# A hybrid HGRN2, convolution and MoE layer: first gather in four passes, x1 kept in DRAM by channels, squares summed on GpSimd, expert input turned by transposes, order of experts first

## Chip, cores and metric

The kernel runs on one core of a Trainium2 chip. The metric is the device time of one execution in microseconds (us), the median of several. In the text PE is TensorE, DVE is VectorE, ACT is ScalarE, POOL is GpSimd, and SP is SyncE, which issues nearly all DMAs. All times inside an execution are counted from the start of the profiled span.

## The reference, cut to what matters

One layer over 256 tokens (128 context tokens, s = 0, and 128 latent tokens, s = 1) of width 1024:

```
h   = rmsnorm(x) * (1 + scale1) + shift1
mix = (g_a * y_a + g_b * y_b) @ w_out                 # HGRN2 branch and convolution branch
x1  = x + gate1 * mix
h   = rmsnorm(x1) * (1 + scale2) + shift2
scores  = sigmoid(h @ w_router)                       # 64 experts, 8 groups
combine = top-8 of the 4 best groups, scores / sum * 2.5
act    = silu(h @ w_gate[e]) * (h @ w_up[e]) * combine[e]      # per expert e, width 256
routed = sum over e of act @ w_down[e]
shared = (silu(h @ ws_gate) * (h @ ws_up)) @ ws_down
out = rmsnorm(x1 + gate2 * (routed + shared)) * final_norm_g
```

Everything is fp32. Each expert has 3 MB of weights, so the 64 experts bring 192 loads of 1 MB.

## The kernel before

**Stages.** The text calls x after the first residual x1. Up to about 392 us the mixers run; their last products are the two halves of the output projection, `project_split("wo0")` and `("wo1")`. DVE adds them to `x_t` (x1 by channels: partition = channel, `[128, 8, 256]`) and writes `h_t` = x1 times the gain of the second norm. Then comes the routing stage, and from about 422 us to 890 us the expert stage, then a short tail (second residual, final norm, store).

**Routing stage on PE** (lines 1793 to 1920). In program order: `sum_squares(j)`, j = 0 to 3, adds the squares of x1 over the channels, four products with a single column each; ACT makes the squares in two buffers `tmp`, and the third and fourth square wait until PE has used the first ones. `sum_squares(0)` stands between the two output projections. Then `router(k)`, k = 0 to 7, the logits (64 columns each); `gained_to_tokens(j)`, 16 products with the identity that turn `h_t` to tokens; `add_shift(j)`, four 512-column products that add the shift row divided by the RMS, in the same PSUM banks; five kinds of small products that count the tokens of each expert (`cnt_ready`); `x1_to_tokens(j)`, 16 transposes of `x_t`, copied by ACT to `x1_out` and stored in DRAM by SP; `gather(part)`, part = 0 to 3, which selects the tokens of the first two steps from `h_hi` and `h_lo` (the expert input split in two fp32r parts) with the one-hot matrix `sel_p`; the product that puts the experts in order (`order_ready`); `turn(0)`.

**DVE there** runs the top-8 selection (up to `mask`), then `h_rest(j)`, which writes `h_lo`, for j = 0 and 1, the positions, `one_hots(0)` (`built`), `h_rest(2)` and `(3)`, the weights `comb`, the keys that rank the experts (`hot_done`), the table of extra slots (`nx_done`), the copy of the order to `e_row` (`order_done`), and two of the four copies of the gathered tokens to `xg`. ACT does the other two.

**Expert stage.** 26 steps; a step takes 1, 2 or 4 experts side by side (`STEPS`). The six experts of the first three steps are fixed, and their weights are loaded before routing is known. Chunk numbers count the loads of 1 MB; there are 18 places in SBUF, and load n goes into the place of load n - 18 once PE has used that (`freed`: `gu_done` for gate and up weights, `dn_done` for down weights). SP issues the loads in that order, so it waits for the release of one place before it issues the next. Chunks 18 and 19 need the order of experts and `gu_done` 1 (first half of `gate_up(0)`); 20 and 21 `gu_done` 2; 22 and 23 `dn_done` 2 (end of `down(0)`); 24 to 27 `gu_done` 3 and 4 (`gate_up(1)`); 28 and 29 `dn_done` 4 (end of `down(1)`).

A step n on PE is: `gate_up(n)` in two halves; `last_results` (scatter of the step before); `act_to_channels(n)`, which waits for ACT's silu and DVE's product `act_r`; `second_turn` or `gather_next`; `down(n)`. In step 0 the small products `before_tables` (which end with `spread2`, the RMS spread over partitions for the shared expert) come after the first half of `gate_up(0)` and `item_tables` after the second.

**Tail.** After the last step DVE signals `loop_done`, PE scatters the last results (8 products), and DVE multiplies by gate2 and adds x1, which SP has loaded back from DRAM behind the last weights.

Release of the places, of the kernel before (the waits that pace the loads):

```
                if part == 2:
                    sp.wait_ge(dn_done, 2 * step + 2)
                else:
                    sp.wait_ge(gu_done, 2 * step + 1 + part)
```

## Time and profile before

| what | us |
|---|---|
| median of 3 runs | 904.22 |
| lowest, highest | 902.78, 906.89 |
| the profiled execution | 905.2 |
| its span | 903.4 |
| PE busy | 831.0 (92%) |
| DVE, ACT, POOL busy | 387.5, 215.3, 91.6 |
| DMA over the span | 284.70 MB, mean 315 GB/s |
| main DMA queue, share of 16 engines' span | 80.5% |
| mean granted TensorE clock | 0.968 |

In a row of the timeline the first two numbers are the start and the time in us, `x16` is the number of instructions merged, and the bracket gives the idle time of the engine before them and who ended it. An fp32 product gives two MATMUL records, an fp32 transpose one. In a row of windows the stretch is followed by its length, the busy time of PE, PEld (weight loads), DVE, ACT and POOL with their instructions, the granted clock of TensorE (1.00 is 2.4 GHz, 0.50 is 1.2 GHz), the DMA share and GB/s.

### The profile page before, as it was taken

How to read it: one execution, taken by the hardware profiler on the slowest of the kernel's cores; microseconds unless marked ns; L12 is line 12 of the kernel's file. 1: busy time of each engine (PE TensorE's matmuls, PEld its weight loads, DVE VectorE, ACT ScalarE, POOL GpSimd, SP SyncE). 2: the span in 40 equal slices, each digit the busy share in tenths (PEclk: the TensorE clock that was granted, in tenths of full speed). 3: DMA queues.
4: the chain of work that ended last, by engine and by line, in shares of the span. 5: the costliest groups of instructions: out<-in, count | busy, mean ns of one | idle time of the engine just before them, and what ended most of it. 6: DMA issues, size and time to landing. Idle time of an engine off the chain costs nothing.

```text
span 903.4 us, 12822 instructions
## 1 busy us (share of the span) xinstructions
PE 831.0 (92%) x5242; PEld 561.4 (62%) x5242; DVE 387.5 (43%) x760; ACT 215.3 (24%) x335; POOL 91.6 (10%) x63
## 2 busy tenths in 40 slices
PE   4699999999899999998999999779999999899973
PEld 2388989569899988995535544435554755345221
DVE  1225898369799846736232322111212111112104
ACT  3124443133354334403111111101111101011001
POOL 1000536205243310000000000000000000000000
PEclk9899999999899999979999999979999999999987
DMA  8979878135234538973999999999999999999993
GB/s 316 386 253 338 309 268 317 39 103 174 67 123 135 193 110 268 410 301 119 377 378 418 418 416 415 418 416 417 416 417 410 418 414 417 417 417 417 418 400 142
DMA packets 81173, 284.70 MB, mean 315 GB/s; under 512 B 5208, under 2 KB 11736, under 8 KB 64728
## 3 DMA queue, kind: packets, MB, share of 16 engines
q1 hardware_dynamic: 80760, 283.11, 80.5%
q8 instruction: 43, 0.70, 0.3%
q10 hardware_dynamic: 352, 0.74, 0.3%
q14 instruction: 18, 0.15, 0.0%
HBM read 280.67 MB, written 3.16 MB: 314 GB/s over the span
## 4 chain that ended last, share of the span: by engine, by line
PE 71%; SPq 12%; DMA 10%; DVE 4%; issue 2%; ACT 0%; POOL 0%; DVEq 0%; POOLq 0%
PE bank L1979 14%; SPq L591 10%; PE bank L2028 8%; PE bank L1588 5%; DMA chunk<-in_w_expert_down 5%; PE bank L1590 5%; PE bank L1596 5%; PE bank L1870 4%; PE bank L1893 4%; PE bank L1576 3%; PE bank L1650 3%; PE bank L1630 3%; DMA ring<-in_w_ada 2%; DMA chunk<-in_w_expert_gate_up 2%; PE bank L1544 2%
## 5 line engine op out<-in xcount | busy, mean ns | idle before, releaser
L1979 PE MATMUL bank<-chunk,xg 128*64 128x512 f32 (+2 forms) x1024 | 200.3, 616 | 21.2 <-DMA chunk<-in_w_expert_gate_up 19.9
L1979 PEld LDWEIGHTS bank<-chunk,xg 128*64 128x64 f32 (+2 forms) x1024 | 62.7, 130 | 153.5 <-issue 137.5
L2028 PE MATMUL bank<-chunk,act_t 128*64 128x512 f32 (+2 forms) x512 | 102.3, 623 | 5.1 <-DMA chunk<-in_w_expert_down 5.0
L1407 DVE SCALAR_TENSOR_TENSOR act_r<-bank,w_slot,sil 128x256 f32<-128x256 f32 x26 | 12.5, 482 | 181.5 <-ACT sil L933 181.5
L645 POOL TENSOR_TENSOR small<-small 128x4 f32<-128x4 f32 (+2 forms) x9 | 10.2, 1138 | 599.2 <-DVE small L1484 501.1
L1419 DVE TENSOR_TENSOR y_lo<-bank,y_hi 128x512 fp32r<-128x512 f32 x52 | 36.0, 691 | 76.4 <-ACT y_hi L946 76.4
L2028 PEld LDWEIGHTS bank<-chunk,act_t 128*64 128x64 f32 (+2 forms) x512 | 31.3, 130 | 54.7 <-issue 53.8
L933 ACT ACTIVATE sil<-bank 128x256 f32<-128x256 f32 x26 | 10.0, 385 | 203.4 <-PE bank L1979 203.4
L1032 DVE TENSOR_TENSOR ring_lo<-ring,ring_hi 128x1024 fp32r<-128x1024 f32 x40 | 47.9, 1220 | 20.4 <-ACT ring_hi L742 20.4
L946 ACT ACTIVATE y_hi<-bank 128x512 fp32r<-128x512 f32 x52 | 31.1, 597 | 105.2 <-PE bank L2028 105.2
L1870 PE MATMUL bank<-sel_p,h_hi 128*128 128x256 f32 x208 | 52.4, 293 | 2.3 <-DVE h_lo L1299 2.3
L1060 DVE SCALAR_TENSOR_TENSOR conv<-upad,dw,conv 128x256 f32<-128x256 f32 x120 | 52.6, 510 | 0.0
L1870 PE MATMUL bank<-sel_p,h_lo 128*128 128x256 f32 x208 | 50.7, 282 | 0.0
L1893 PE MATMUL bank<-y_hi,sel_t 128*128 128x512 f32 x104 | 44.8, 431 | 2.3 <-DVE small L1466 2.3
L1032 DVE TENSOR_TENSOR w_lo<-ring,w_hi 128x1024 fp32r<-128x1024 f32 x28 | 33.8, 1248 | 30.6 <-ACT w_hi L742 30.6
L742 ACT ACTIVATE ring_hi<-ring 128x1024 fp32r<-128x1024 f32 x40 | 40.4, 1049 | 19.5 <-PE bank L1615 14.8
L1870 PEld LDWEIGHTS bank<-sel_p,h_hi 128*128 128x128 f32 x208 | 39.4, 189 | 3.0 <-issue 2.5
L1377 DVE COPY xg<-bank 128x512 f32<-128x512 f32 x26 | 17.9, 690 | 54.4 <-PE bank L1870 54.4
L1893 PE MATMUL bank<-y_lo,sel_t 128*128 128x512 f32 x104 | 40.9, 394 | 0.0
L1870 PEld LDWEIGHTS bank<-sel_p,h_lo 128*128 128x128 f32 x208 | 39.6, 190 | 0.0
L1650 PE MATMUL bank<-qk,k_mix 128*128 128x128 f32 x224 | 31.4, 297 | 5.3 <-issue 4.8
L1893 PEld LDWEIGHTS bank<-y_hi,sel_t 128*128 128x128 f32 x104 | 19.5, 187 | 24.9 <-issue 18.2
(293 smaller groups left out, 1323.2 us busy)
## 6 DMA issues: line engine op xcount, KB each, us to landing
chunk<-in_w_expert_gate_up SPq DMA_DIRECT2D x128, 1024.0 KB, 20.6
chunk<-in_w_expert_down SPq DMA_DIRECT2D x64, 1024.0 KB, 22.6
ring<-in_w_in SPq DMA_DIRECT2D x16, 2048.0 KB, 10.6
ring<-in_w_ada SPq DMA_DIRECT2D x12, 2048.0 KB, 13.4
ring<-in_w_proj_hgrn SPq DMA_DIRECT2D x2, 2048.0 KB, 8.1
ring<-in_w_out SPq DMA_DIRECT2D x2, 2048.0 KB, 13.5
ring<-in_w_proj_conv SPq DMA_DIRECT2D x1, 2048.0 KB, 7.8
chunk<-in_w_shared_gate_up SPq DMA_DIRECT2D x2, 1024.0 KB, 23.4
```

Source lines behind the costliest of these rows:

```text
L591: sp.dma_start(dst, src).then_inc(s_chunk[place], 16)
L742: nc.scalar.activation(part_hi(n, q), tile_of(split[n])[:, :, q * P:(q + 1) * P], ACT.Copy).then_inc(w_hi_done, 1)
L1032: V.tensor_tensor(part_lo(n, q), tile_of(split[n])[:, :, q * P:(q + 1) * P], part_hi(n, q).bitcast(F32), ALU.subtract).then_inc(w_lo_done, 1)
L1060: ins = V.scalar_tensor_tensor(dst, src, tap, dst, ALU.mult, ALU.add)
L1588: mm(out, part_hi(n, q)[:, k, :], h1_hi[:, k, :], start=(k == 0), stop=False)
L1590: mm(out, part_lo(n, q)[:, k, :], h1_hi[:, k, :], start=False, stop=False)
L1596: ins = mm(out, part_hi(n, q)[:, k, :], (h1_lo if n < apart else h1_rest)[:, k, :], start=False, stop=(k == KD - 1))
L1650: ins = mm(out, k_mix[:, at_ * P:(at_ + 1) * P], query_mix(level, at_), start=True, stop=True)
L1870: ins = mm(bank[part % banks][:, c * 2 * P:(c + 1) * 2 * P], src[:, s, k, :], sel_p[:, s, :], start=(n == 0), stop=(n == 3))
L1893: ins = mm(y_acc[s][h][:, :], sel_t[b][:, s * P:(s + 1) * P], part[h][:, :], start=(first and part is y_hi), stop=(last and part is y_lo))
L1979: ins = mm(bank[2 + b][row:row + width, :], xg[:, k, c:c + width], w[:, k % 4, :], start=(k == 0), stop=(k == KD - 1))
L2028: ins = mm(out[row:row + width, :], act_t[:, c, row:row + width], w[:, c, h * 512:(h + 1) * 512], start=(c == 0), stop=(c == 1))
```

## The change

- **Squares.** POOL adds the first three squares of x1 (`sq_sum`); PE sums over the channels twice instead of four times, between `router(3)` and `router(4)`, and nothing stands between the output projections.
- **Expert input.** `gained_to_tokens` uses transposes (`is_transpose=True`) in place of products with the identity. `add_shift` still adds to them.
- **x1.** `x1_to_tokens`, ACT's four copies and SP's store leave the routing stage. ACT issues a store of `x_t` as it is, after its fourth square. At the end SP loads it back (`x1_back`, first of the closing loads, before gate2 and the final gain); PE turns it by 16 transposes, eight ahead of the last scatter and eight behind it, ACT copies them to `x1`, and DVE's residual waits for the copies. `xg`, `fin`, `g2row` and place 17 change addresses for it.
- **First gather.** Four passes (context hi, latent hi, context lo, latent lo) over four banks, each started when its input is there. DVE does only `h_rest(0)` ahead of the positions.
- **Order.** DVE ranks the experts before it makes the weights, and copies the order before it copies gathered tokens; the extra-slot table comes after both. `turn(0)` moves between the halves of `gate_up(0)`, `before_tables` behind its second half, `item_tables` between the halves of `gate_up(1)`; DVE's `tables()` and `items()` move likewise. Each half of `gate_up` waits only for its own half of `xg`. SP reads an expert's number just before its first load.

The diff, cut:

```
+            for j in (1, 2):
+                pool.wait_ge(x1_sq, j + 1)
+                first = tmp[:, 0, :] if j == 1 else sq_sum[:, :]
+                if j > 1:
+                    pool.wait_ge(sq_summed, j - 1)
+                nc.gpsimd.tensor_tensor(sq_sum[:, :], first, tmp[:, j % 2, :], ALU.add).then_inc(sq_summed, 1)
...
                 if j >= 2:
-                    act.wait_ge(ssq2_ready, j - 1)
+                    act.wait_ge(sq_summed, 1)
...
+            act.dma_start(A["x1"], x_t[:, :, :].rearrange("p k t -> p (k t)")).then_inc(s_x1_kept, 16)
...
-                    mm(b[:, i * P:(i + 1) * P], h_t[:, 4 * hf + i, s * P:(s + 1) * P], ident, start=(i == 0), stop=False)
+                    mm(b[:, i * P:(i + 1) * P], h_t[:, 4 * hf + i, s * P:(s + 1) * P], ident, start=(i == 0), stop=False, is_transpose=True)
...
-            sum_squares(0)
             project_split("wo1", m_hi, m_lo, m_hi_done, m_lo_done)
-            sum_squares(1)
-            sum_squares(2)
-            sum_squares(3)
-            pe.wait_ge(brow_done, 1)
-            for k in range(KD):
+            pe.wait_ge(b_copied, 2)
+            for k in range(4):
+                router(k)
+            pe.wait_ge(sq_summed, 2)
+            pe.wait_ge(o_copied, 4)
+            sum_squares(sq_sum, True, False)
+            pe.wait_ge(x1_sq, 4)
+            sum_squares(tmp[:, 1, :], False, True)
+            for k in range(4, KD):
                 ins = router(k)
...
-            x1_to_tokens(0)
-            x1_to_tokens(1)
-            x1_to_tokens(2)
-            x1_to_tokens(3)
...
             pe.wait_ge(built, 1)
+            pe.wait_ge(lg_done, 1)
+            pe.wait_ge(h_hi_done, 2)
+            first_gather(0, 0, h_hi)
+            pe.wait_ge(h_hi_done, 4)
+            first_gather(1, 1, h_hi)
+            evacuated(pe, "hr", 1)
+            first_gather(2, 0, h_lo)
             evacuated(pe, "hr", 3)
-            for part in range(4):
-                gather(part, 4)
+            first_gather(3, 1, h_lo)
...
-                    if n == 0:
-                        (item_tables if half else before_tables)()
+                    if (n, half) == (0, 0):
+                        pe.wait_ge(weights_done, 1)
+                        pe.wait_ge(gbk_evac, 2)
+                        pe.wait_ge(ga_evac, 2)
+                        turn(0, weights_of(0))
+                    if (n, half) == (0, 1):
+                        before_tables()
+                    if (n, half) == (1, 0):
+                        item_tables()
...
             pe.wait_ge(loop_done, 1)
+            x1_to_tokens(0)
+            x1_to_tokens(1)
             for s in range(NS):
                 for h in range(2):
                     ins = scatter(1, s, h, last=True)
                 ins.then_inc(y_done, 1)
+            x1_to_tokens(2)
+            x1_to_tokens(3)
```

On PE, behind the output projection, the kernel before has the squares (L1799), the router (L1807), the turn of the expert input (L1815) and the added shift (L1821):

```order
L1799 MATMUL bank<-ones,tmp 128x1 x12
L1807 MATMUL bank<-w_r,h_t 128x64 x16
L1815 MATMUL bank<-consts,h_t 128x128 x16
L1821 MATMUL bank<-shift_row,diag_inv 128x512 x4
L1899 MATMUL bank<-rt,consts 128x64
```

The changed kernel has there:

```order
L1818 MATMUL bank<-w_r,h_t 128x64 x8
L1810 MATMUL bank<-ones,sq_sum 128x1 x4
L1810 MATMUL bank<-ones,tmp 128x1 x4
L1818 MATMUL bank<-w_r,h_t 128x64 x8
L1826 MATMUL bank<-consts,h_t 128x128 x16
L1832 MATMUL bank<-shift_row,diag_inv 128x512 x4
L1902 MATMUL bank<-rt,consts 128x64
```

Half of the router moved ahead of the squares, of which 8 products are left here, and the turn keeps its count but is now in transpose form.

On DVE, from `h_rest` to the first weights, before (L1299 is `h_rest`, L1264 `one_hots`, L1338 the first of the weights):

```order
L1299 SCALAR_TENSOR_TENSOR h_lo<-bank,small,h_hi 128x64x8 [waits h2_hi_done,proj_ready]
L1299 SCALAR_TENSOR_TENSOR h_lo<-bank,small,h_hi 128x64x8 [waits h2_hi_done]
L1332 SCALAR_TENSOR_TENSOR rt<-bank,rt 128x128 [waits count_ready,mask_done]
L1333 TENSOR_SCALAR pos_f<-rt 128x12 [waits own_dve]
L1264 TENSOR_TENSOR sel_p<-consts_x,pos_f 128x256 [waits routing_consts_loaded,own_dve]
L1264 TENSOR_TENSOR sel_p<-consts_x,pos_f 128x256
L1299 SCALAR_TENSOR_TENSOR h_lo<-bank,small,h_hi 128x64x8 [waits h2_hi_done] x2
L1338 TENSOR_TENSOR rt<-rt 128x128
```

And now, where L1348 to L1352 are the keys, L1353 to L1357 the weights, L1360 the order and L1346 the copies of gathered tokens (rows left out between the fences' parts):

```order
L1304 SCALAR_TENSOR_TENSOR h_lo<-bank,small,h_hi 128x64x8 [waits h2_hi_done,proj_ready]
L1336 SCALAR_TENSOR_TENSOR rt<-bank,rt 128x128 [waits count_ready,mask_done]
L1269 TENSOR_TENSOR sel_p<-consts_x,rt 128x256 [waits router_and_routing_consts_loaded,own_dve]
L1269 TENSOR_TENSOR sel_p<-consts_x,rt 128x256
L1304 SCALAR_TENSOR_TENSOR h_lo<-bank,small,h_hi 128x64x8 [waits h2_hi_done,proj_ready] x3
L1348 SCALAR_TENSOR_TENSOR rt<-bank,consts 64x64
...
L1352 TENSOR_SCALAR rt<-consts_x,rt 64x58 [waits own_dve]
L1353 TENSOR_TENSOR rt<-rt 128x128
...
L1360 CAST e_row<-bank 1x58 [waits expert_order_ready]
L1346 COPY xg<-bank 128x512 [waits gather_b] x2
```

One `h_rest` moved behind the one-hot matrices, and keys, weights, order and copies follow in that order.

On PE at the end of the first step, before, behind `gate_up(0)` come the item tables (L1940 to L1944), then `act_to_channels` (L2019):

```order
L1979 MATMUL bank<-chunk_100,xg 64x512
L1940 MATMUL bank<-rt,tmp 128x94
L1941 MATMUL bank<-rt 128x94
L1942 MATMUL bank<-rt,tmp 128x94
L1940 MATMUL bank<-rt,tmp 128x94
L1941 MATMUL bank<-rt 128x94
L1942 MATMUL bank<-rt,tmp 128x94
L1943 MATMUL bank<-rt,consts 1x36
L1944 MATMUL bank<-ones,rt 1x1
L2019 MATMUL bank<-consts,act_r 128x128 x2
```

Now `before_tables` (L1934 to L1941) stands there, with the spread of the RMS as its last product:

```order
L1988 MATMUL bank<-chunk_100,xg 64x512
L1934 MATMUL bank<-rt,consts 64x1
L1936 MATMUL bank<-consts,rt 64x128
L1937 MATMUL bank<-consts,rt 64x128
L1936 MATMUL bank<-consts,rt 64x128
L1937 MATMUL bank<-consts,rt 64x128
L1941 MATMUL bank<-diag_140,ones 128x256
L2035 MATMUL bank<-consts,act_r 128x128 x2
```

On ACT the copy of that spread (`inv2`) still stands ahead of the first table load and the first silu.

## Rows read from the trace of the kernel before

**Rows 1.** Timeline, SP's DMA issues: the first ranked loads

```profile
426.00 16.75 SPq L591 DMA_DIRECT2D chunk<-in_w_expert_gate_up  x8
445.34 11.56 SPq L591 DMA_DIRECT2D chunk<-in_w_expert_down  x4
```

**Rows 2.** Busy time by windows, around and in the expert stage

```profile
450.00:460.00 10.00, 10.00 (x55) 4.56 (x55) 2.72 (x7) 1.79 (x3) 0.00 (x0) 1.00 0.85 320
460.00:470.00 10.00, 10.00 (x56) 4.67 (x56) 3.36 (x10) 1.96 (x4) 0.00 (x0) 1.00 1.03 427
...
600.00:700.00 100.00, 99.63 (x502) 52.02 (x504) 22.68 (x54) 16.57 (x32) 0.00 (x0) 0.98 1.02 415
```

**Rows 3.** Timeline, PE, routing stage: squares, router, turn, shift, transposes of x1

```profile
391.84 1.84 PE L1799 MATMUL bank<-ones,tmp 128*128 128x1 f32 x16
...
394.80 7.01 PE L1807 MATMUL bank<-w_r,h_t 128*128 128x64 f32 x32
401.60 5.47 PE L1815 MATMUL bank<-consts,h_t 128*128 128x128 f32 x32
406.91 3.60 PE L1821 MATMUL bank<-shift_row,diag_inv 128*128 128x512 f32 x8
...
411.66 2.00 PE L1831 MATMUL bank<-consts,x_t 128*128 128x128 f32 x16
```

**Rows 4.** Busy time by windows: where TensorE's clock fell, rose and held

```profile
394.00:396.00 2.00, 2.00 (x14) 2.00 (x15) 0.78 (x9) 0.00 (x0) 0.70 (x1) 0.72 0.94 377
...
404.00:406.00 2.00, 2.00 (x15) 2.00 (x14) 1.82 (x11) 0.00 (x0) 0.00 (x0) 0.72 1.03 424
...
414.00:416.00 2.00, 0.04 (x1) 0.07 (x1) 2.00 (x3) 0.42 (x1) 0.00 (x0) 1.00 0.35 143
...
585.00:587.00 2.00, 0.00 (x0) 0.00 (x0) 0.00 (x0) 0.00 (x0) 0.00 (x0) 0.75 1.00 418
...
883.00:884.00 1.00, 1.00 (x12) 0.41 (x8) 0.00 (x0) 0.00 (x0) 0.00 (x0) 0.50 0.81 269
...
886.00:887.00 1.00, 1.00 (x12) 0.36 (x8) 0.58 (x1) 0.38 (x1) 0.00 (x0) 0.81 1.01 414
```

**Rows 5.** Timeline, DVE: mask, h_rest twice, keys, last key, copies of gathered tokens

```profile
407.48 0.29 DVE L1326 TENSOR_TENSOR rt<-rt 128x128 f32<-128x128 f32 x1
410.55 2.13 DVE L1299 SCALAR_TENSOR_TENSOR h_lo<-bank,small,h_hi 128x512 fp32r<-128x512 f32 x2 [2.78 <-PE bank L1821]
...
413.76 2.06 DVE L1299 SCALAR_TENSOR_TENSOR h_lo<-bank,small,h_hi 128x512 fp32r<-128x512 f32 x2
...
416.90 0.21 DVE L1344 SCALAR_TENSOR_TENSOR rt<-bank,consts 64x64 f32<-64x64 f32 x1
...
417.74 0.24 DVE L1348 TENSOR_SCALAR rt<-consts_x,rt 64x58 f32<-64x58 f32 x1
...
420.78 1.27 DVE L1377 COPY xg<-bank 128x512 f32<-128x512 f32 x2
```

**Rows 6.** Chain of waits, in order of time, at the first gather

```profile
415.96 4.07 PE bank L1870 x32
```

**Rows 7.** Timeline, PE: first half of gate_up(0), act_to_channels(0), gate_up(1)

```profile
422.15 3.65 PE L1979 MATMUL bank<-chunk,xg 128*64 128x512 f32 x16 [1.22 <-issue]
...
433.65 0.44 PE L2019 MATMUL bank<-consts,act_r 128*128 128x128 f32 x2 [1.38 <-DVE act_r L1407]
...
438.11 7.07 PE L1979 MATMUL bank<-chunk,xg 128*64 128x512 f32 x32
```

**Rows 8.** Timeline, ACT: table load and first silu

```profile
427.44 1.28 ACT L933 ACT_TABLE_LOAD   x1
430.63 0.39 ACT L933 ACTIVATE sil<-bank 128x256 f32<-128x256 f32 x1 [1.91 <-PE bank L1979]
```

**Rows 9.** Timeline, PE: the last scatter

```profile
890.17 0.50 PE L1893 MATMUL bank<-y_hi,sel_t 128*128 128x512 f32 x1 [2.33 <-DVE small L1466]
```

**Rows 10.** Timeline, POOL: the shortest of its 1024-column products

```profile
306.50 1.94 POOL L682 TENSOR_TENSOR qk<-qk,fg 128x1024 f32<-128x1024 f32 x1 [10.18 <-PE bank L1650]
```

212 lines of the change are left out of this document (107 added, 105 removed).

## The prediction

> **What bounds the kernel now.** I read the time from its end. In the expert stage the DMA engines are full: 415 GB/s over the hundred us from 600, and 427 already at 460 [rows 2]. So the end of the stage is the moment from which the loads never stop again, plus a fixed amount of bytes. That moment is the release of chunks 28 and 29 at the end of `down(1)`, 455.7: in 450 to 460 the rate is still 320 GB/s [rows 2], and before it SP hands out its loads in pairs as PE frees places, 8 gate-up loads over 16.75 us and 4 down loads over 11.56 us where four megabytes would need 10 us at full rate [rows 1]. Whatever PE gains up to `down(1)` therefore comes out at the end one for one; what it gains later doesn't.
>
> Going back from there along PE: `gate_up(0)` starts at 422.15 [rows 7], after copies of the gathered tokens on DVE (420.78) [rows 5], after a gather of 4.07 us that waits for the last `h_rest` (413.76 + 2.06 = 415.8) [rows 5, 6], which waits for the counts and the added shift (406.91 to 410.3), after the turn (401.60), the router (394.80) and the squares (391.84) [rows 3]. The clock matters in it: it falls to 0.50 near 395, three us into the one-column products, and is back at 405 [rows 4].
>
> **The change, step by step** (times in the span of 903.4; the execution took 905.2).
>
> *1. Squares and router.* 16 records of squares took 1.84 us, 0.115 each [rows 3]. The four products ahead of the second projection half go: 8 records, 0.9, so PE begins here at 390.9. Now come 16 records of router, at the full clock 1.9 by the squares' 0.115 (the router's own 7.01 / 32 = 0.22 [rows 3] was paid at half clock [rows 4], and half of it is 0.11), then 16 of squares, 1.9, to 394.7, then 16 of router. The one-column stretch is shorter than the one that dropped the clock (1.9 against 3.0 us) and is framed by router products; but these didn't lift the clock in 6.7 us at half, so I count them as light work too and expect the fall still to come, near 395 to 396: 3.0 us for the second half, logits at 397.7 instead of 401.8. Bounds 3.5 (398.2) and 1.9 (396.6). POOL's two adds of 512 columns take some 1 us each by its 1.94 for 1024 columns [rows 10]; the first has 5 us until ACT's third square needs it, the second 4 us until PE does. They cost nothing; uncovered, 1 us.
>
> *2. Turn.* 32 records become 16. At full clock transposes took 2.00 us for 16 [rows 3], at half 16 x 0.22 = 3.5: 397.7 to 401.1. The shift's four products need 3.45 at full clock (406.91 to 410.3); the clock was back some 3.5 us after dense work began (401.60 to 405) [rows 3, 4], so here near 402.5, costing 0.7. End of shift 405.3 instead of 410.3: **5.0 gained**. The mask comes 6 us after the logits (407.8 against 401.8 [rows 5]), so at 403.7, still ahead of it. Bounds: with the clock kept the mask decides, 402.7, and 7.5 are gained; with the clock at half throughout the shift 3.3.
>
> At this place the Trainium skill speaks against the change. What the rows show: the clock stayed 1.00 in 414 to 416, where PE did nothing, right behind 2.0 us of transposes [rows 3, 4]; the last dense products, those of the shift, had ended at 410.3, 5.6 us before PE's next work at 415.96 [rows 3, 6]. That is longer than the 3 us of one-column products that dropped the clock at 395, so the transposes seem to have counted. TensorE: Matmul & The Clock Gate, Part 4 (PE-mode transpose), says that a transpose does not count as a busy PE in the way a product does. The held clock speaks against that rule; its case is a rival below.
>
> *3. Counts to h_rest.* Counts took 1.3 us to 411.7: now to 406.6. DVE has done `h_rest(0)` (1.03, from 2.13 and 2.06 for two [rows 5]) by then. Positions and one-hots 1.1: 407.7. Three `h_rest`, 3.1: 410.8 against 415.8. Before, two `h_rest` ended at 412.6, 0.9 behind the counts, and two more followed the one-hots; now one ends ahead of the counts and three follow. The two cancel: still **5.0**.
>
> *4. Gather, keys, order, copies.* Only the last of four passes (4.07 / 4 = 1.0 [rows 6]) follows the last `h_rest`, but DVE is later: keys 1.1 (416.90 to 417.98), weights 1.1 (415.8 to 416.9), order 0.2, one copy of 512 columns 0.64 [rows 5]: 410.8 + 3.1 = 413.9 for the start of `gate_up(0)` against 422.15 [rows 7]. **8.2 gained.** The 2.0 us of `x1_to_tokens` [rows 3] lay beside DVE's work; taking them out gives nothing more.
>
> *5. First step.* Before, from that start to `act_to_channels(0)` 11.5 us (433.65) [rows 7]. Now two halves 7.3, `turn` 0.7, `before_tables` 1.2: 9.2. But ACT's copy of the spread RMS stands ahead of its table load, and the spread is now the last thing PE does there. So after 9.2: copy 0.4 (as a silu of the same 256 columns), table load 1.28, silu 0.39 [rows 8], DVE 0.5: 11.8. The table load, hidden before, is bare; PE idles 2.7 us instead of 1.38 [rows 7]. Minus 0.3. `item_tables` (1.7, formerly inside the 11.5) now sits in `gate_up(1)`, which took 7.0 [rows 7]. Minus 1.7. **6.2 gained** at the end of `gate_up(1)`, and at `down(1)`. The earlier releases gain 6 to 8.5; the queue runs dry between them as before. The order is known at 413.3, 4 us before `gate_up`'s first half frees a place, so reading experts singly costs nothing (if the cover went, 0.5 a load).
>
> *6. Loads of chunk 17 and the store of x1* fall into the time before 417, when the DMA engines had idle time: nothing. Uncovered, 1 MB each at 415 GB/s [rows 2], 2.5.
>
> *7. Tail.* PE starts the last scatter at 890.17 on DVE's `loop_done` [rows 9]. Eight transposes now precede it: 1.0 [rows 3], all exposed. The other eight and ACT's copies are ready before the second residual. Bounds 0.9 and, at half clock, 1.8. **1.0 lost.**
>
> Sum: 905.2 - 6.2 + 1.0 = 900.0. The profiled execution stands 1.0 above the median of the runs (904.22) and inside their spread; I take off half of that: **899.5**.
>
> **Rivals.** *A. The new gap drops the clock.* In this trace the clock fell in 585 to 587 behind an idle of over 2 us and held in 414 to 416 [rows 4], so with 2.7 us idle in the first step it can go either way. Price: at 883 it fell and was back in 886 [rows 4], 3.4 us at half speed, 1.7 lost, passed on in full: 901.2. Against: more PE work stands around the gap.
>
> *B. The clock holds through the router,* because the squares are half as many and split from the mixers' dense work by router products: step 2's 7.5 instead of 5.0: 897.0. Against: the router kept it at half for 6.7 us without raising it [rows 3, 4].
>
> *C. Transposes don't count as work.* Then the turn doesn't lift the clock, and nearly all of the shift runs at half: 1.7 later, 901.2. The Trainium skill's sentence above would make it so.
>
> *D. Slower: the clock again.* The change takes dense products out (half of the turn) and opens gaps at four places: the wait for the one-hots, the 2 us before `gate_up(0)`, the 2.7 behind it, and the tail. At 1.7 a fall, three falls eat the 5.2; with four it is slower than before: 906.3. It decides at the third. For: each gap is near the length that dropped it. Against: the kernel before has gaps of 2.3 and 1.4 there and kept its clock.
>
> *E. Less arrives than PE gains:* the queue is already what paces the first ranked loads, or x1's load, now waited for by PE, lands late. Two thirds of the gain lost: 903.
>
> **How the numbers follow.** Forecast (899.5, own range 898 to 901) 0.45; A 0.26; B 0.12; C 0.05; D 0.05; E 0.07. Range 896.0 (B with 1 us) to 903.5 (E, and A twice); it leaves D and little else outside. A measurement of this kernel tells 0.5% from no change, that is 4.5 us, so faster means under 899.7. The forecast sits on that edge: half of it, a little more than B, and a share for luck in A and C make 0.45 faster; 0.49 same; 0.06 slower.
>
> **What would show it.** Right: logits near 397.7 and a half clock after 395; start of `gate_up(0)` at 414; an idle PE of 2.7 us behind `before_tables`, ended by `act_r`, with ACT's table load in it; rate full from about 449; the last weights at 876; 1 us of transposes before the scatter. Wrong: `gate_up(0)` later than 416, a DMA rate under 400 after 460, or PE waiting for x1's load.

## The result, and the profile after

The changed kernel takes 900.15 us (median; 893.97 to 903.74), the kernel before 905.06 in the same comparison: ratio 0.9947, 95% interval 0.9929 to 0.9964. A second comparison gave 900.28 against 904.4, ratio 0.9953 (0.9931 to 0.9975). So it is faster by about half a per cent, 4 to 5 us. The prediction was 899.5, and its range of 896.0 to 903.5 holds the result. The profiled execution took 899.69, with a span of 897.9. Its total is as foretold; how it comes about is not, and that is what the experiments are about.

PE behind the second output projection, answering [rows 3]; columns as there:

```profile
387.98 1.90 PE L1818 MATMUL bank<-w_r,h_t 128*128 128x64 f32 x16
389.71 1.00 PE L1810 MATMUL bank<-ones,sq_sum 128*128 128x1 f32 x8
390.58 1.03 PE L1810 MATMUL bank<-ones,tmp 128*128 128x1 f32 x8
391.47 3.65 PE L1818 MATMUL bank<-w_r,h_t 128*128 128x64 f32 x16
394.91 3.58 PE L1826 MATMUL bank<-consts,h_t 128*128 128x128 f32 x16
398.32 3.60 PE L1832 MATMUL bank<-shift_row,diag_inv 128*128 128x512 f32 x8
...
404.40 3.19 PE L1914 MATMUL bank<-sel_p,h_hi 128*128 128x256 f32 x16 [1.25 <-DVE sel_p L1269]
407.39 2.58 PE L1914 MATMUL bank<-sel_p,h_lo 128*128 128x256 f32 x16
```

Everything here lies 2.9 us earlier than foretold, since the router starts at 387.98 and not at 390.9. Measured from the router's start the steps are those of the prediction: logits after 6.9 (6.8 foretold), end of the shift after 13.8 (14.4), `gate_up(0)` after 23.1 (23.0). The first step, answering [rows 7]:

```profile
411.10 3.65 PE L1988 MATMUL bank<-chunk,xg 128*64 128x512 f32 x16 [0.94 <-ACT xg L924]
...
419.65 0.60 PE L1941 MATMUL bank<-diag,ones 128*128 128x256 f32 x2
422.93 0.69 PE L2035 MATMUL bank<-consts,act_r 128*128 128x128 f32 x2 [2.69 <-DVE act_r L1416]
...
424.62 5.82 PE L2044 MATMUL bank<-chunk,act_t 128*64 128x512 f32 x16
```

`act_to_channels(0)` comes 11.83 us behind `gate_up(0)`, with 2.69 us of idle (11.8 and 2.7 foretold). ACT in that gap, answering [rows 8]: the copy of the spread RMS, then the bare table load, then silu.

```profile
420.28 0.38 ACT L929 ACTIVATE inv<-bank 128x256 f32<-128x256 f32 x1 [9.90 <-PE bank L1941]
420.68 1.28 ACT L934 ACT_TABLE_LOAD   x1
421.98 0.38 ACT L934 ACTIVATE sil<-bank 128x256 f32<-128x256 f32 x1
```

The next lines are windows (busy time of PE, PEld, DVE, ACT, POOL, then granted clock, DMA share, GB/s), answering [rows 4] and [rows 2]:

```profile
405.00:406.00 1.00, 1.00 (x8) 1.00 (x7) 1.00 (x2) 0.00 (x0) 0.00 (x0) 0.57 1.02 418
408.00:409.00 1.00, 1.00 (x9) 1.00 (x8) 0.90 (x5) 0.00 (x0) 0.00 (x0) 0.72 0.27 94
...
422.00:424.00 2.00, 1.07 (x6) 1.07 (x6) 1.47 (x8) 0.70 (x2) 0.00 (x0) 0.55 1.02 422
428.00:430.00 2.00, 2.00 (x10) 0.70 (x8) 0.69 (x1) 0.60 (x1) 0.00 (x0) 0.74 0.00 0
...
447.00:450.00 3.00, 3.00 (x16) 0.99 (x14) 0.69 (x1) 1.09 (x2) 0.00 (x0) 1.00 0.18 74
450.00:460.00 10.00, 10.00 (x50) 4.68 (x48) 1.96 (x6) 0.87 (x3) 0.00 (x0) 1.00 0.94 367
```

The clock fell in the gap, at 422.2, and stayed low through `down(0)`, which took 5.82 us: rival A. It had also fallen inside the gather, from 405.1 to 408.6, which no step of the prediction has. The DMA engines then twice have nothing to do (427 to 431 and 448 to 450); they start again as `down(1)` ends, 449.4, and are full from 452 on.

### The profile page after: what moved, and what is told of

It reads as the page before. It is cut to its first block, busy times and chain, and to the rows that moved or that the text cites. A ratio compares the mean times of both kernels' runs of the same rounds, so it can differ in the third digit from the quotient of the medians.

```text
span 897.9 us, 12790 instructions
## 1 busy us (share of the span) xinstructions
PE 830.5 (93%) x5210; PEld 558.2 (62%) x5210; DVE 385.9 (43%) x759; ACT 215.4 (24%) x335; POOL 101.9 (11%) x65
## 4 chain that ended last, share of the span: by engine, by line
PE 60%; SPq 22%; DMA 9%; DVE 5%; issue 3%; ACT 1%; POOL 0%; DVEq 0%; POOLq 0%; ACTq 0%
SPq L593 20%; PE bank L1988 9%; PE bank L2044 5%; DMA chunk<-in_w_expert_down 5%; PE bank L1602 5%; PE bank L1604 5%; PE bank L1610 5%; PE bank L1590 3%; PE bank L1644 3%; PE bank L1558 3%; PE bank L1664 3%; DMA chunk<-in_w_expert_gate_up 2%; PE bank L1873 2%; PE bank L1896 2%; PE bank L1625 2%
## 5 line engine op out<-in xcount | busy, mean ns | idle before, releaser
L1988 PE MATMUL bank<-chunk,xg 128*64 128x512 f32 (+2 forms) x1024 | 202.9, 626 | 20.3 <-DMA chunk<-in_w_expert_gate_up 19.3
L2044 PEld LDWEIGHTS bank<-chunk,act_t 128*64 128x64 f32 (+2 forms) x512 | 31.2, 130 | 54.8 <-issue 54.0
L1873 PE MATMUL bank<-sel_p,h_hi 128*128 128x256 f32 x192 | 48.5, 293 | 0.0
L1873 PE MATMUL bank<-sel_p,h_lo 128*128 128x256 f32 x192 | 46.8, 282 | 0.0
L750 ACT ACTIVATE ring_hi<-ring 128x1024 fp32r<-128x1024 f32 x40 | 40.4, 1050 | 19.5 <-PE bank L1629 15.2
L1346 DVE COPY xg<-bank 128x512 f32<-128x512 f32 x26 | 17.9, 690 | 54.4 <-PE bank L1873 54.4
L666 POOL TENSOR_SCALAR fg<-fg,small 128x256 f32<-128x256 f32 x16 | 26.7, 1670 | 103.2 <-ACT qk L783 103.2
L1873 PEld LDWEIGHTS bank<-sel_p,h_hi 128*128 128x128 f32 x192 | 36.3, 189 | 0.5
L1873 PEld LDWEIGHTS bank<-sel_p,h_lo 128*128 128x128 f32 x192 | 36.5, 190 | 0.0
```

The costliest lines, as they stand in the source:

```text
L750: nc.scalar.activation(part_hi(n, q), tile_of(split[n])[:, :, q * P:(q + 1) * P], ACT.Copy).then_inc(w_hi_done, 1)
L1873: ins = mm(bank[part % 2][:, c * 2 * P:(c + 1) * 2 * P], src[:, s, k, :], sel_p[:, s, :], start=(n == 0), stop=(n == 3))
L1988: ins = mm(bank[2 + b][row:row + width, :], xg[:, k, c:c + width], w[:, k % 4, :], start=(k == 0), stop=(k == KD - 1))
L2044: ins = mm(out[row:row + width, :], act_t[:, c, row:row + width], w[:, c, h * 512:(h + 1) * 512], start=(c == 0), stop=(c == 1))
```

## Where the time of an execution goes

Fourteen profiles were taken: of before, of the changed kernel twice and of eleven variants. Each span is the sum of P and five stretches, read from PE's timeline. P is the end of the second output projection (in before and in `squares_again` less the 0.9 us of squares that stand ahead of it). The stretches run from there to `gate_up(0)`; on to `act_to_channels(0)`; on to the end of `down(1)`; on to the start of the last `down`, which waits for the last weights; and from there to the end.

The medians come from four comparisons, each with executions of the kernel before beside its own: the changed kernel first (before 905.1); `changed_again`, `inv2_late`, `tail_early` and `products_again` (before 904.4); `gap_filled`, `tail_ahead`, `best` and `squares_again` (before 904.8); and `one_pass`, `tables_back`, `scatter_first` and `clock_held` (before 902.7). The changed kernel itself stands in the first two alone. Across comparisons, therefore, the ratios to before are to be compared, not the medians.

| kernel | median | P | to gate_up(0) | to act (0) | to down(1)'s end | to last down | to the end |
|---|---|---|---|---|---|---|---|
| before | 902.7 to 905.1 | 390.9 | 31.2 | 11.5 | 21.85 | 427.0 | 20.9 |
| changed | 900.2 | 388.0 | 23.1 | 11.8 | 26.5 | 426.8 | 21.7 |
| changed_again | 900.3 | 390.8 | 21.5 | 11.8 | 26.65 | 426.6 | 21.7 |
| products_again | 900.8 | 391.1 | 24.3 | 13.5 | 25.2 | 426.9 | 20.3 |
| squares_again | 901.0 | 390.9 | 26.9 | 11.8 | 26.6 | 426.7 | 21.7 |
| one_pass | 905.1 | 390.9 | 26.6 | 11.8 | 26.4 | 426.9 | 21.5 |
| tables_back | 901.4 | 391.1 | 24.4 | 13.2 | 23.4 | 426.7 | 23.25 |
| gap_filled | 896.6 | 389.9 | 21.5 | 11.8 | 23.7 | 426.6 | 21.5 |
| inv2_late | 893.5 | 388.6 | 21.5 | 9.0 | 23.6 | 426.7 | 24.2 |
| tail_early | 896.3 | 386.9 | 23.1 | 11.8 | 23.65 | 426.8 | 21.5 |
| tail_ahead | 900.2 | 389.7 | 23.1 | 11.8 | 26.4 | 426.85 | 21.3 |
| best | 895.1 | 393.0 | 23.1 | 9.0 | 23.7 | 426.65 | 20.6 |
| scatter_first | 896.2 | 389.8 | 21.5 | 9.0 | 23.7 | 426.6 | 24.4 |
| clock_held | 894.4 | 389.4 | 23.15 | 9.0 | 23.7 | 426.5 | 21.4 |

Four things are to be seen. **The column of 426.5 to 427.0** is the prediction's "one for one": `down(1)` ends anywhere between 442.7 and 456.3, and the last weights come 426.8 us later, give or take 0.25. **Some stretches have two values** in the nine profiles that are alike from the router to `gate_up(0)` (the changed kernel's two, `gap_filled`, `inv2_late`, `tail_early`, `tail_ahead`, `best`, `scatter_first` and `clock_held`): 23.1 or 21.5 to `gate_up(0)`, and some 26.5 or 23.65 behind `act_to_channels(0)`. That is TensorE's clock, which falls early or late, and falls or holds. In `products_again` and `tables_back` it falls at other places, and they lie between or below (25.2 and 23.4). **P varies by 6 us** over kernels that do the same up to there. And one profile is one draw of all of these: a median of many executions tells a change in them, a single span does not.

## Experiments

**The changed kernel again.**

> The changed kernel as it is, to stand beside its variants on the same chip, with a second profile. Theory 1 (the gain is made between the router and down(1), 3.1 us in the profile, and the other 3.0 us by which this profile runs ahead before the router are an accident of the first 80 us, where the clock was 0.92 to 0.96 before and 0.96 to 1.00 after): the router starts between 388 and 391, anywhere in it, and the ratio is again 0.993 to 0.996. Theory 2 (something in the change also speeds up the stages ahead of the router, as the loads): the router starts at 388 again, and in all variants of the changed kernel too. Both: gate_up(0) starts 23 us behind the router's first product, act_to_channels(0) 11.8 us behind that, PE idle 2.7 us ahead of it, and the clock at 0.50 from about 422 to 429 if the fall there is the rule and not chance.

Median 900.28 (12 runs), span 899.0. P is 390.8: the 2.9 us by which the first profile ran ahead of the router are chance (theory 1). The variants, all but `squares_again` the same up to there, spread from 386.9 to 393.0. The time is lost early: one and the same product of the mixers starts between 83.3 (`tail_early`) and 89.3 (`best`), and from it to P all fourteen profiles need 302.7 to 304.3 us. A window of before, of `tail_early` and of `best`:

```profile
40.00:60.00 20.00, 19.04 (x83) 14.87 (x84) 9.77 (x22) 7.18 (x12) 0.00 (x0) 0.83 0.70 253
```

```profile
40.00:60.00 20.00, 20.00 (x111) 16.43 (x110) 9.60 (x16) 7.55 (x12) 0.00 (x0) 0.95 0.87 309
```

```profile
40.00:60.00 20.00, 17.42 (x79) 14.60 (x76) 10.55 (x26) 5.67 (x9) 0.00 (x0) 0.88 0.64 237
```

At 253, 309 and 237 GB/s P is 390.9, 386.9 and 393.0. Which comes first, slow loads or a slow PE that frees the ring late, no run here tells. Against the loads speaks that in 20 to 40 all profiles moved 386 or 387 GB/s, while the granted clock there read from 0.50 (`best`) to 1.00 (the changed kernel's first profile).

The clock's falls are not independent draws either. The four profiles with 21.5 in the table, in which the fall at the router came late, are the four whose granted clock in 230 to 240 read 0.83; in the other ten it read 0.66 to 0.79. What ties places 150 us apart together, no run tells.

The fall in the gap was there again (`down(0)` 5.95 us, clock 0.50 in 424 to 426). `gate_up(0)` starts 21.5 us behind the router's start and not 23, as the clock fell later at the router.

**The spread's copy moved behind the first silu.**

```diff
-            act.wait_ge(spread2, 1)
-            nc.scalar.activation(inv2[:, :], bank[7][:, 0:T], ACT.Copy).then_inc(inv2_done, 1)
...
                 gate(n % 2, n)
+                if n == 0:
+                    act.wait_ge(spread2, 1)
+                    nc.scalar.activation(inv2[:, :], bank[7][:, 0:T], ACT.Copy).then_inc(inv2_done, 1)
```

> The changed kernel with ACT's copy of the spread RMS (inv2) moved from ahead of the first silu to behind the first copy of act_t. Nothing is left out. Theory 1 (the copy held back the table load, the bare load and copy make PE's 2.7 us of idle, the idle drops the clock, which costs down(0) another 2.2 us: 5.82 against 3.65 us, and what PE gains up to down(1) arrives at the end one for one): act_to_channels(0) starts 9.3 to 9.6 us behind gate_up(0) instead of 11.8, idle under 0.4 us, down(0) in 3.65 us, down(1) ends 4 to 5 us earlier, and the time is 3.5 to 5 us shorter: 895 to 896.5. Rival a (the clock falls there anyway, because of the light work around it): 2.4 us shorter. Rival b (the loads are paced by SP's queue and not by PE any more): act_to_channels earlier as in theory 1, but the last weights land less than 1.5 us earlier and the time is 0 to 1.5 us shorter.

893.5 us (891.77 to 895.51), ratio to before 0.9864 (0.9837 to 0.989), against 0.9953 for the changed kernel beside it: 6.8 us less. ACT first, then PE:

```profile
409.42 1.28 ACT L932 ACT_TABLE_LOAD   x1
418.12 0.38 ACT L932 ACTIVATE sil<-bank 128x256 f32<-128x256 f32 x1 [7.42 <-PE bank L1989]
...
419.83 0.38 ACT L954 ACTIVATE inv<-bank 128x256 f32<-128x256 f32 x1
```

```profile
418.67 0.60 PE L1942 MATMUL bank<-diag,ones 128*128 128x256 f32 x2
419.10 0.41 PE L2036 MATMUL bank<-consts,act_r 128*128 128x128 f32 x2
...
420.08 3.65 PE L2045 MATMUL bank<-chunk,act_t 128*64 128x512 f32 x16
```

The table load lies under the first half of `gate_up(0)`, silu starts as the second half ends, PE has no gap and `down(0)` full speed. `down(1)` ends 54.1 us behind P, against 61.5 and 60.0. Theory 1 holds, and rival a, which would have given 2.4 us, is out; the size is above the 3.5 to 5 us foretold. Of the 6.8 the profiles account for 5.8: 2.85 for the idle and 2.95 for the clock, which costs more than its 2.2 us in `down(0)` (next run). The last 1.0 us lies within what five executions leave open. Rival b is out: the last weights come 426.7 us behind `down(1)` as ever.

**The gap filled with products**, the idle left as long as it was:

```diff
                         before_tables()
+                        for _ in range(5):
+                            mm(bank[1][:, 0:T], ones[:, :], diag2[:, :], start=True, stop=True)
```

> The changed kernel with five products of 256 columns more behind before_tables, from the same operands as the spread, into a bank that nobody reads then (some 0.46 us each, 2.3 in all), so that PE works in the 2.7 us in which it waits for act_r. Nothing is left out. What separates the idle from the clock: act_to_channels(0) starts as before, 11.8 us behind gate_up(0). Theory 1 (the idle drops the clock in part of the executions and then costs 2.2 us at down(0)): down(0) takes 3.65 us, the clock stays 1.00 from the fillers to 430, and the median is 1 to 2.2 us under that of the changed kernel (900.2), 898 to 899.2, with fewer runs above 901. Theory 2 (the idle doesn't drop the clock, light work ahead of it does, or the two fast variants owe their gain to something else): down(0) again in 5.8 us in the profile, the median as the changed kernel's, within 0.7.

896.6 us (890.86 to 900.76), ratio 0.9903 (0.9871 to 0.9936). Its profile and that of `changed_again` are twins up to `act_to_channels(0)` (21.5 and 11.8 in the table). Behind it:

```profile
420.36 2.32 PE L2008 MATMUL bank<-diag,ones 128*128 128x256 f32 x10
423.21 0.44 PE L2037 MATMUL bank<-consts,act_r 128*128 128x128 f32 x2 [0.53 <-DVE act_r L1416]
...
424.21 3.65 PE L2046 MATMUL bank<-chunk,act_t 128*64 128x512 f32 x16
```

and in `changed_again`:

```profile
424.12 0.69 PE L2035 MATMUL bank<-consts,act_r 128*128 128x128 f32 x2 [2.69 <-DVE act_r L1416]
...
425.81 5.95 PE L2044 MATMUL bank<-chunk,act_t 128*64 128x512 f32 x16
```

Theory 1: work without use keeps the clock, at 1.00 from the fillers to 430, and from `act_to_channels(0)` to the end of `down(1)` it takes 23.7 instead of 26.65. So a fall here costs 2.9 to 3.0 us, 2.3 in `down(0)` and 0.7 in what stands between `act_to_channels` and it (1.7 us against 1.0), and the idle itself another 2.85 (11.83 less 8.98): the 5.8 us of `inv2_late`. The medians alone would not carry this: 3.6 us were gained where 1 to 2.2 were foretold, and `tail_early` below stands as low at six executions, by an edit that moved 0.2 us. What carries it is the pair of profiles.

**The turn as plain products.**

```diff
-                    mm(b[:, i * P:(i + 1) * P], h_t[:, 4 * hf + i, s * P:(s + 1) * P], ident, start=(i == 0), stop=False, is_transpose=True)
+                    mm(b[:, i * P:(i + 1) * P], h_t[:, 4 * hf + i, s * P:(s + 1) * P], ident, start=(i == 0), stop=False)
```

> The changed kernel with the turn of x1*g written as plain products with the identity again (32 records instead of 16). Nothing is left out. Theory 1 (a transpose counts for the clock like a product): the clock comes back 3.3 us behind the turn's first product, as it did behind the first transpose (394.91 to 398.2), the turn takes 5.2 to 5.4 us instead of 3.4, the shift 3.45, and gate_up(0) starts 1.8 us later; the time is 1.5 to 2.2 us longer. Theory 2 (transposes don't count, and the clock came back in the changed kernel for another reason, as by chance of phase): with products the clock comes back at another distance from the turn's start, earlier by 1 us or more, and the loss is under 1 us. Theory 3 (rule out the turn as critical: the mask or h_rest decides): the loss is under 0.5 us at the start of gate_up(0).

900.78 us, ratio 0.9953 (0.993 to 0.9977): no difference that the times can tell, where theory 1 had 1.5 to 2.2 us. In its profile the turn took 5.6 us against 3.2 to 3.4, and the shift ended 15.6 us behind P against 13.8 and 12.2, so the records cost what theory 1 says; `gate_up(0)` came after 24.3. That the median shows none of it I can't explain but by the falls, which lie elsewhere here (the gather ran at full clock, 4.3 us; `gate_up(0)`'s first half took 5.35). Left open.

On what it was made for, the run is clear: the clock came back 4.2 us behind the turn's first product here and 3.5 in before, and 3.4, 3.7 and 2.65 behind its first transpose in the changed kernel's two profiles and in `tail_early` (up to 4.1 in the others). That last one, PE's timeline and windows:

```profile
394.15 3.20 PE L1826 MATMUL bank<-consts,h_t 128*128 128x128 f32 x16
397.20 3.60 PE L1832 MATMUL bank<-shift_row,diag_inv 128*128 128x512 f32 x8
```

```profile
394.00:396.00 2.00, 2.00 (x11) 2.00 (x11) 1.20 (x10) 0.89 (x3) 0.00 (x0) 0.50 0.98 406
396.00:397.00 1.00, 1.00 (x8) 1.00 (x7) 0.96 (x14) 0.00 (x0) 0.00 (x0) 0.60 1.01 426
397.00:398.00 1.00, 1.00 (x6) 0.58 (x5) 0.90 (x5) 0.00 (x0) 0.00 (x0) 1.00 1.07 451
```

The clock rose at 396.8, before the shift's first product and after nothing but router products and 2.65 us of transposes. By the Trainium skill's rule (TensorE: Matmul & The Clock Gate, Part 4 (PE-mode transpose)) a transpose doesn't count as a busy PE in the way a product does; the traces here speak against it for transposes of 128x128 in fp32, and rival C is out.

**All squares on PE again**, in the old order and without POOL's adds, on PE:

```diff
+            sum_squares(0)
             project_split("wo1", m_hi, m_lo, m_hi_done, m_lo_done)
+            sum_squares(1)
+            sum_squares(2)
+            sum_squares(3)
             pe.wait_ge(b_copied, 2)
-            for k in range(4):
-                router(k)
...
-            sum_squares(sq_sum, True, False)
-            pe.wait_ge(x1_sq, 4)
-            sum_squares(tmp[:, 1, :], False, True)
-            for k in range(4, KD):
+            for k in range(KD):
                 ins = router(k)
```

> The changed kernel with all four squares summed on PE, where the kernel before had them (one ahead of the second output projection, three behind it, then the router), and without POOL's adds. Nothing is left out. Theory 1 (by the records: 8 of 0.115 us behind the projection and 8 ahead of it, and the clock falls in the one-column products in either order): from the end of the second projection to the first transpose of the turn 9.0 us, against 6.9 and 5.3 in the two profiles of the changed kernel; last weights 1.5 to 3.5 us later, time 901.5 to 903.5. Theory 2 (the router's first half only moves the light work about, and the clock falls as often): 0.9 to 1.8 longer. Rival (POOL's adds hold up ACT's third square and cost what they save): the same time within 0.5.

900.98 us, ratio 0.9964 (0.9947 to 0.9981). In the profile the turn starts 10.6 us behind P, 6.75 of it in the router at half clock, against 6.9 and 5.3: 3.7 us or more, as step 1 has it (theory 1). But that execution took 906.4 us, the slowest of twelve, and the median is only 0.7 to 0.8 over the changed kernel's (theory 2). What the step is worth stays open between the two; where the clock stood in the usual execution no profile shows.

**The gather's passes all behind the last h_rest.**

```diff
-            pe.wait_ge(h_hi_done, 2)
+            pe.wait_ge(h_hi_done, 4)
+            evacuated(pe, "hr", 3)
             first_gather(0, 0, h_hi)
-            pe.wait_ge(h_hi_done, 4)
             first_gather(1, 1, h_hi)
-            evacuated(pe, "hr", 1)
             first_gather(2, 0, h_lo)
-            evacuated(pe, "hr", 3)
             first_gather(3, 1, h_lo)
```

> The changed kernel with all four passes of the first gather behind the last h_rest, the rest as it is (also the order of its products). Nothing is left out. Measured from the router's first product, which starts at 387 to 393 by chance. Theory 1 (three of four passes lie beside h_rest, and PE is what the copies wait for): the gather starts 3.1 us later (19.5 us behind the router's start where the changed kernel has 16.4, or 17.9 where it has 14.8), takes 4.1 at full clock, and gate_up(0) starts 1.5 to 2.2 us later (24.7 to 25.3 against 23.1, or 23.0 to 23.7 against 21.5). Theory 2 (DVE, with keys, weights and the order, is the bound, since it waited only 0.6 us for PE there): 0.6 us later at most... that is, gate_up(0) under 23.9 (or 22.3). Time by theory 1: 901 to 903 at a median of 900.2 for the changed kernel; by theory 2 within 0.8.

905.08 us beside 902.73 for before, ratio 1.0018 (1.0002 to 1.0035), with 901 to 903 foretold: all of the change's gain is gone. This is the one part of the change that the times show by itself.

```profile
410.40 3.75 PE L1914 MATMUL bank<-sel_p,h_hi 128*128 128x256 f32 x16 [4.29 <-DVE h_lo L1304]
413.95 2.46 PE L1914 MATMUL bank<-sel_p,h_lo 128*128 128x256 f32 x16
416.34 0.26 PE L1927 MATMUL bank<-rt,consts 64*1 64x58 f32 x2
417.54 3.65 PE L1986 MATMUL bank<-chunk,xg 128*64 128x512 f32 x16 [0.94 <-ACT xg L924]
```

The gather starts 19.5 us behind the router's start, as theory 1 said, but takes 5.9 us and not 4.1: PE had idled 4.29 us and the clock was down (0.50 from 408 to 414). `gate_up(0)` comes after 26.6, which is 3.5 and 5.1 later than in the changed kernel's two profiles; 1.5 to 2.2 were expected, as I had set a gather at full clock against one at half. Theory 2 is out: DVE now waits 4.22 us for the order.

**Turn and tables back where they were**, on PE (DVE's `tables` and `items` moved likewise, ahead of its loop):

```diff
+                if n == 0:
...
+                    turn(0, weights_of(0))
                 for half in range(2):
...
-                    if (n, half) == (0, 0):
...
-                        turn(0, weights_of(0))
-                    if (n, half) == (0, 1):
-                        before_tables()
-                    if (n, half) == (1, 0):
-                        item_tables()
+                    if n == 0:
+                        (item_tables if half else before_tables)()
```

> The changed kernel with the work around gate_up(0) where the kernel before had it: turn ahead of gate_up(0), before_tables behind its first half, item_tables behind its second, DVE's part of them ahead of act_r. ACT's copy of the spread RMS and its table load are then hidden by gate_up's second half again. Nothing is left out. Theory 1 (step 5 of the prediction: the move makes the 2.7 us of idle and only shifts item_tables' 1.7 us into gate_up(1)): gate_up(0) starts 0.7 to 1.0 us later, act_to_channels(0) about 11.5 us behind it, idle 1.4, down(0) in 3.65 us, item_tables' time gone from gate_up(1); down(1) ends 57 to 58 us behind the router's start, against 61.4 and 60.0 in the two profiles of the changed kernel and 58.6 in the one of its variants in which the clock held; time 896 to 898.5, so this part of the change costs 2 to 4 us. Theory 2 (the move is worth what it was made for, since gate_up's loads are freed earlier and the queue needs that): the last weights land more than 427.5 us behind the end of down(1), and the time is within 1 us of the changed kernel's or longer.

901.43 us (894.83 to 903.86), ratio 0.9969 (0.9947 to 0.9991) against 0.9947 and 0.9953 for the changed kernel. My theory 1 foretold 896 to 898.5 and fell: nothing is gained. Its idle of 1.38 us and the hidden table load are there. But `gate_up(0)` starts 1.3 us later, not 0.7 to 1.0, and the clock falls at other places:

```profile
414.81 0.41 PE L1876 MATMUL bank<-consts,sel_p 128*128 128x128 f32 x2 [1.54 <-DVE xg L1346]
415.06 0.51 PE L1879 MATMUL bank<-rt,sel_p 128*128 128x2 f32 x4
415.49 5.31 PE L1985 MATMUL bank<-chunk,xg 128*64 128x512 f32 x16
...
429.96 4.91 PE L2039 MATMUL bank<-chunk,act_t 128*64 128x512 f32 x16
```

With both halves of `gate_up(0)` and `down(0)` at 3.65 it would be 61.0 - 1.65 - 1.25 = 58.1 us from P to the end of `down(1)`, against 58.6 in `tail_early`, where the changed kernel's order ran without a fall in the gap. So by this reckoning, which no run shows, the two orders are nearly even; what the change lost in the first step it lost to where ACT's copy stands, since `inv2_late` with the new order has 54.1.

**The tail, three times.** First, the wait for `loop_done` behind the first eight transposes:

```diff
-            pe.wait_ge(loop_done, 1)
             x1_to_tokens(0)
             x1_to_tokens(1)
+            pe.wait_ge(loop_done, 1)
```

> The changed kernel with PE's first eight transposes of x1 ahead of its wait for loop_done, so in the 2.3 us in which it waits for DVE, instead of behind it. Nothing is left out. Theory 1 (these transposes are 1.0 us of exposed work at the end): the last scatter starts straight behind loop_done, and the time is 0.8 to 1.1 us shorter. Theory 2 (the end is set by something else, as ACT's copies of x1 or its squares): 0 to 0.4 us shorter. Theory 3 (x1 lands only after the last down): PE waits for it and the time is the same or longer; in the profile of the changed kernel it had landed at 878.6, and the last down ended at 881.5, which speaks against it.

896.29 us (895.24 to 898.58, six runs), ratio 0.9906 (0.9881 to 0.9932). That is 4.0 us under `changed_again` beside it, and the edit doesn't explain it: from the start of the last `down` to the end the profile has 21.5 us, the changed kernel's two 21.7. In the profile itself a short P (386.9) and a gap without a fall make it fast. Whether chance alone did the same in five more executions stays open, and with it how far a median of six can be trusted to 4 us. In the profile x1 had landed at 874.6, `down` ended at 875.9, and still:

```profile
872.27 3.64 PE L2044 MATMUL bank<-chunk,act_t 128*32 128x512 f32 x32 [1.52 <-DMA chunk<-in_w_expert_down]
878.27 1.97 PE L2104 MATMUL bank<-consts,x_back 128*128 128x128 f32 x8 [2.36 <-issue]
```

The transposes wait 2.36 us for nothing that a semaphore shows. Between the last `down` and them lie the reading of `nwork` and the branch over the extra experts. `loop_done` came at 878.13, so the branch ended 0.1 us behind it and the edit could win next to nothing. Second, then, they were put ahead of that branch, ACT's two copies too:

```diff
+            x1_to_tokens(0)
+            x1_to_tokens(1)
             n_extra = pe.value_load(nwork, min_val=0, max_val=NX)
             with pe.If(n_extra > 0):
+                pe.wait_ge(x1_copied, 2)
                 gather_next(NIT - 1, extra_weights(0))
```

> The changed kernel with PE's first eight transposes of x1 straight behind the last down, ahead of the reading of nwork and the branch over the extra experts, and ACT's two copies of them ahead of ACT's branch. Nothing is left out. When the transposes stood behind the branch but ahead of the wait for loop_done they began 2.36 us behind the last down, not behind its end, with x1 landed 1.3 us before that end: so PE's branch, not only DVE, holds PE for 2.3 us. Theory 1 (the branch holds PE, and the transposes are exposed behind it): they start within 0.2 us of the end of the last down, the scatter starts 2.3 to 3.4 us behind that end instead of 3.2 (the changed kernel), i.e. the branch's 2.3 us now begins 1.0 later and nothing is gained there (0 to 0.3 us), unless PE passes the branch while its products run. Theory 2 (PE's sequencer reads ahead, and it is DVE's loop_done that sets the scatter): the scatter starts 2.4 us behind the last down and 1.0 us is gained: time 0.8 to 1.2 under the changed kernel's at the same clock, span from the start of the last down to the end 20.7 instead of 21.7. Both readings are made from that span, since the median moves with the clock by more than this.

900.2 us, ratio 0.9954: the changed kernel's.

```profile
883.07 1.09 PE L2089 MATMUL bank<-consts,x_back 128*128 128x128 f32 x8
885.98 0.50 PE L1900 MATMUL bank<-y_hi,sel_t 128*128 128x512 f32 x1 [1.82 <-DVE small L1484]
```

The transposes follow `down` at once, and the scatter starts 0.6 us behind `loop_done` (885.36), where in the changed kernel it starts 1.0 behind it, with the transposes between: from the last `down`'s start to the end 21.3 instead of 21.7. PE's branch takes its 1.8 to 2.4 us after whatever stands ahead of it. Theory 1. With both,

> inv2_late and tail_ahead together. Nothing is left out. Expected by theory 1 (PE up to down(1) counts one for one: the last weights land 426.6 us behind the end of down(1), as in all profiles so far): the 893.5 of inv2_late less 0 to 1.2: 892.3 to 893.5. If the two interfere, as by a later clock fall at the end: 893.5 to 895.

895.09 us (892.74 to 899.5), ratio 0.9892 (0.9864 to 0.9919): not better than `inv2_late` alone, and above the 892.3 to 893.5 expected. Here `down` ran at full clock and ended early, and the branch alone held the scatter, 1.5 us behind `loop_done` (881.24):

```profile
878.96 1.09 PE L2090 MATMUL bank<-consts,x_back 128*128 128x128 f32 x8
882.77 0.50 PE L1901 MATMUL bank<-y_hi,sel_t 128*128 128x512 f32 x1 [2.72 <-issue]
```

Third, on top of `inv2_late`, the transposes behind the first sample's scatter:

```diff
-            x1_to_tokens(0)
-            x1_to_tokens(1)
             for s in range(NS):
                 for h in range(2):
                     ins = scatter(1, s, h, last=True)
                 ins.then_inc(y_done, 1)
+                if s == 0:
+                    x1_to_tokens(0)
+                    x1_to_tokens(1)
```

> inv2_late with PE's first eight transposes of x1 behind the scatter of the first sample instead of ahead of it. Nothing is left out. From loop_done on: scatter 0.9 us, then the transposes 1.1 beside DVE's gated_y of 1.3 us, copies 0.6 behind each half. Theory 1 (only DVE's chain counts, and it waits 0.3 to 0.5 us for x1's copies): from the start of the last down to the end 21.0 to 21.2 us with the clock at 0.50 in that down (21.7 in the two profiles of the changed kernel, 5.3 us in the down), 19.4 to 19.6 with it at 1.00; time 0.5 to 0.7 under inv2_late's 893.5. Theory 2 (the second sample's scatter, now 1.1 us later, is waited for by DVE): no gain, 893.5 within 0.4.

896.2 us (893.56 to 898.67). In the profile the transposes ran at half clock (1.91 us), so that x1 came late after all; DVE:

```profile
881.28 1.28 DVE L1490 TENSOR_TENSOR fin<-g2row,bank 128x512 f32<-128x512 f32 x2 [1.86 <-PE bank L1897]
883.62 1.23 DVE L1495 TENSOR_TENSOR fin<-fin,x 128x1024 f32<-128x1024 f32 x1 [1.05 <-ACT x L970]
```

From `loop_done` to the end 15.5 us, `inv2_late` 15.4: nothing gained, if by another wait than theory 2 names. The median lies above what either theory allowed. Last, products against the clock's fall ahead of the last `down`:

```diff
+                if n == NSTEPS - 1:
+                    for _ in range(10):
+                        mm(bank[1][:, 0:P], ident, ident, start=True, stop=True)
                 down(n)
```

> scatter_first with ten products of 128 columns (identity by identity, some 2.3 us in all) into a bank that is free then, ahead of the last down, where PE waits 2.7 us for the last weights. Nothing is left out. Theory 1 (the idle ahead of the last down drops the clock; it took 5.2 to 5.3 us in five of the profiles and 3.64 in three): down takes 3.64 us always and the time is 0 to 1.7 under scatter_first's, on average 1.0: 891.5 to 892.5. Theory 2 (the clock falls all the same, as DMA-bound stages leave PE little to do): down again in 5.3 in the profile, and no difference. Rival: the products run past the landing and delay down by up to 0.5 us.

```profile
868.57 2.40 PE L2082 MATMUL bank<-consts 128*128 128x128 f32 x20
871.72 3.64 PE L2045 MATMUL bank<-chunk,act_t 128*32 128x512 f32 x32 [0.76 <-DMA chunk<-in_w_expert_down]
```

`down` takes 3.64 us where `scatter_first` had 6.60, and the last stretch 21.4 instead of 24.4. 894.38 us (890.67 to 897.13), 1.8 less, though the intervals (0.9874 to 0.9922, 0.9903 to 0.9945) overlap, and above the 891.5 to 892.5 expected. The clock still fell behind `down`, 0.72 in 876 to 882.

The four kernels with `inv2_late` in them have medians of 893.5 to 896.2, and all beat both kernels. The three that add to it are not told apart. `inv2_late` alone (0.9837 to 0.989) and `scatter_first` (0.9903 to 0.9945) have intervals that don't meet, though their profiles differ by 0.1 us behind `loop_done`; they come from two comparisons, and nothing here explains the difference.

## The prediction, step by step

*What bounds the kernel:* right, and the firmest of it. All fourteen profiles have 426.5 to 427.0 us from the end of `down(1)` to the last weights.

*1 and 2, squares, router, turn:* the sizes held (6.9 and 13.8 us behind the router's start). The clock fell and came back about 1 us earlier than foretold (3.5 and 10.3 us behind the router's start in the first profile, for 4 to 5 and 11.6). In four of nine profiles with this front it fell some 2 us later (5.5 us behind the router's start, not 3.1 to 3.9), stayed down for half as long, and `gate_up(0)` came 1.6 us earlier: two thirds of rival B's 2.5. *3 and 4, one-hots, gather, copies:* 23.1 against 23.0. The gather's term was wrong in itself: behind the last `h_rest` came not one pass of 1.0 us but two, 2.5 us at half clock (407.39 to 409.97). It did little harm, because DVE, with the weights ready at 409.6, was nearly as late and waited only 0.62 us for PE. `products_again`, whose gather ran at full clock, has 6.0 us from its start to `gate_up(0)`, the changed kernel 6.7. `one_pass` shows that without the four passes nothing of the gain is left.

*5, first step:* 11.83 against 11.8 and then 23.65 without a fall against 21.85 in before, 1.8 lost where 1.7 was foretold. What failed is rival A's place in the account: the sum holds no fall in the gap, and the usual execution has one. I took it as a chance of 0.26 at a price of 1.7; of the seven profiles that keep the idle unfilled six show a longer `down(0)` (4.69 to 5.95; the seventh, `tail_early`, 3.65), and it costs 2.9. With it `down(1)` ends 61.5 us behind P, 3.1 less than before and not 6.2. The reading that failed is the price from the row at 883 [rows 4]: it counted some 3.4 us of half speed, while here they are 6.8, from 422.2 to 429.0. Falls of the longer kind stood in the kernel before too (0.50 from 869.3 to 876), beside the one that was read.

*6:* nothing measured speaks against it. *7, tail:* 1.0 foretold, 0.8 measured (14.15 from `loop_done` to the end against 13.35). But I had put the 2.33 us ahead of the scatter [rows 9] down to DVE alone; PE's own branch ends at nearly the same moment.

*The sum:* foretold were 6.2 gained up to the end of `down(1)`, which puts it 58.4 us behind P for 64.6 in before. The late falls at the router (four of nine, 1.6 us each) take 0.7 off that, and the falls in the gap (six of seven, 2.9 us each) add 2.5: 60.2 us, and 4.4 gained. Less the tail's 0.8 that is 3.6, an estimate from few profiles; the medians say 4.1 and 4.9. The first profile's 5.5 holds 2.9 of chance ahead of the router. So the number came out right partly by luck: the rivals A and B were both in part true, and partly cancelled. Rival D, slower, was far off, though falls came: from the router to `down(1)` before has one (394.9 to 405.05), the first profile of the changed kernel three (391.5 to 398.3, 405.1 to 408.6, 422.2 to 429.0). The first is shorter than before's, the second cost some 0.7 us, and only the third costs what D feared, and more.
